# Expert loop of a Conformer and mixture-of-experts layer: where TensorE reads the expert classes, where the large experts stand in the sequence, and the order of TensorE's first turns

## The reference

```python
mod = silu(c) @ ada_w + ada_b                      # (1, 6*D): six vectors sh1, sc1, g1, sh2, sc2, g2
h = rmsnorm(x, mix_norm_g) * (1 + sc1) + sh1
u = h @ pw1_w + pw1_b; u = a * sigmoid(gt)         # a, gt: the halves of u
u = causal_depthwise_conv(u, dw_w, dw_b)           # 31 taps
y = silu(layernorm(u)) @ pw2_w + pw2_b;  x = x + g1 * y
h = rmsnorm(x, ffn_norm_g) * (1 + sc2) + sh2
top_val, top_idx = top_k(h @ router_w + router_b, 4)   # 4 of 32 experts for each token
for each expert e and its tokens xk:
    g, u = split(xk @ w1[e] + b1[e]);  act = (clip(u)+1) * (min(g,7) * sigmoid(1.702*g))
    y = act @ w2[e] + b2[e]                        # added to each token, weighted by its gate
x = x + g2 * moe;  out = rmsnorm(x, final_norm_g)
```

## Time and profile before

| what | value |
|---|---|
| device time, median of 3 runs | 1222.03 us (1221.42 to 1222.82) |
| device time of the profiled execution | 1223.35 us, of which 1221.5 us are the span from the first to the last instruction |
| TensorE matmuls busy | 1019.1 us, 83% of the span |
| DVE, ACT, POOL busy | 333.4, 165.4, 7.1 us |
| read from HBM | 455.9 MB, 374 GB/s over the span |
| chain of work that ended last | TensorE 64%, DMA 22%, issue 6%, DVE 5% |
| mean granted TensorE clock | 0.928 of full |

### The profile page before, as it was taken

The page is one execution under the profiler, slowest core; times in us unless marked ns, Lnnn a source line. Parts: engine busy times, 40 slices in busy tenths (PEclk is TensorE's granted clock), DMA queues, the critical chain, the costliest instruction groups (busy, mean ns, idle before and its releaser), DMA issues.

```text
span 1221.5 us, 20933 instructions
## 1 busy us (share of the span) xinstructions
PE 1019.1 (83%) x7648; PEld 476.7 (39%) x7649; DVE 333.4 (27%) x876; ACT 165.4 (14%) x364; POOL 7.1 (1%) x19
## 2 busy tenths in 40 slices
PE   3899994988899989998999799988787777877774
PEld 2577472333444334433443344333233323332321
DVE  3344457222113211231123112222121212121213
ACT  2233433010101010101010101010101010101001
POOL 1000000000000000000000000000000000000000
PEclk9999996899999988999999889989798989898988
DMA  9962990899999999999999998999999999999992
GB/s 353 280 276 102 334 389 19 335 421 421 421 395 386 421 422 382 374 422 422 414 382 421 422 409 339 422 423 423 421 422 421 423 421 422 422 422 422 422 421 110
DMA packets 84813, 457.39 MB, mean 374 GB/s; under 512 B 9497, under 2 KB 30097, under 8 KB 30993
## 3 DMA queue, kind: packets, MB, share of 16 engines
q1 hardware_dynamic: 83184, 456.29, 92.6%
q10 hardware_dynamic: 1600, 0.71, 0.2%
HBM read 455.93 MB, written 1.05 MB: 374 GB/s over the span
## 4 chain that ended last, share of the span: by engine, by line
PE 64%; DMA 22%; issue 6%; DVE 5%; ACT 1%; ACTq 1%; SPq 0%; DVEq 0%
PE bank L1226 29%; DMA ring<-in_exp_w 21%; PE bank L1249 15%; PE bank L1098 5%; PE bank L1205 3%; PE bank L1080 2%; PE bank L1119 2%; PE bank L1046 2%; PE bank L1217 2%; DMA xg<-in_conf_dw_w 1%; PE bank L1236 1%; DVE scratch L877 1%; PE bank L1203 1%; PE bank L1193 1%; DVE act L887 1%
## 5 line engine op out<-in xcount | busy, mean ns | idle before, releaser
L1226 PE MATMUL bank<-ring,xg 128*32 128x256 f32 (+2 forms) x3136 | 452.4, 484 | 42.9 <-DMA ring<-in_exp_w 42.6
L1226 PEld LDWEIGHTS bank<-ring,xg 128*32 128x32 f32 (+2 forms) x3136 | 175.2, 130 | 309.7 <-issue 206.0
L1249 PE MATMUL bank<-ring,actT 128*32 128x512 f32 (+2 forms) x1056 | 224.0, 622 | 24.2 <-DMA ring<-in_exp_w 16.1
L525 ACT ACTIVATE act<-scratch 128x128 f32<-128x128 f32 (+2 forms) x66 | 25.8, 391 | 810.2 <-DVE scratch L877 808.8
L1249 PEld LDWEIGHTS bank<-ring,actT 128*32 128x32 f32 (+2 forms) x1056 | 77.3, 135 | 147.6 <-issue 114.5
L866 DVE SCALAR_TENSOR_TENSOR acc<-bank,gate,acc 128x512 f32<-128x512 f32 x136 | 93.0, 744 | 81.0 <-PE bank L1205 71.8
L877 DVE TENSOR_SCALAR scratch<-bank 128x128 f32<-128x128 f32 (+2 forms) x66 | 25.6, 388 | 306.0 <-PE bank L1226 306.0
L896 DVE TENSOR_TENSOR ysb<-bank,g2half 128x512 f32<-128x512 f32 x29 | 20.1, 692 | 226.2 <-PE bank L1249 226.2
L1193 PEld LDWEIGHTS bank<-onehot_bf,arena 128*128 128x128 bf16 x1584 | 54.4, 100 | 22.0 <-issue 22.0
L1217 PE MATMUL bank<-b1s,bias_of 96*32 96x256 bf16 (+2 forms) x196 | 25.5, 375 | 43.6 <-issue 43.6
L1098 PE MATMUL bank<-hT,ring 128*128 128x256 f32 x256 | 58.6, 389 | 3.7 <-DVE wcol L645 3.7
(11 more groups left out here) (214 smaller groups left out, 513.1 us busy)
## 6 DMA issues: line engine op xcount, KB each, us to landing
ring<-in_exp_w SPq DMA_DIRECT2D x396, 1024.0 KB, 22.3
ring<-in_ada_w SPq DMA_DIRECT2D x24, 1024.0 KB, 9.9
ring<-in_conf_pw_w SPq DMA_DIRECT2D x12, 1024.0 KB, 11.4
acc<-in_x SPq DMA_DIRECT2D x1, 1024.0 KB, 5.0
out<-acc SPq DMA_DIRECT2D x2, 512.0 KB, 2.6
g2full<-in_ada_b SPq DMA_DIRECT2D x1, 512.0 KB, 4.6
xT<-in_final_norm_g ACTq DMA_DIRECT2D x1, 512.0 KB, 3.9
b1f<-in_exp_b SPq DMA_DIRECT2D x1, 256.0 KB, 4.2
```

The costliest lines, as they stand in the source:

```text
L525: a.activation(act[:, h * c:(h + 1) * c], g_lim[h][:, 0:c], ACT.Sigmoid, scale=ALPHA).then_inc(sig_ready, 1)
L1226: ins = mm(up_to(m, n, r), xg[:, b, k, 0:m], wk[:, at:at + span(m)], start=False, stop=(k == KT - 1))
L1249: ins = mm(dst, actT[:, f % (2 * q), at:at + m], wk[:, f % 2 * D + r * H:f % 2 * D + (r + 1) * H], start=(f < sides), stop=(f >= KT - sides))
```

## The change

- The first turns of TensorE are reordered: x is transposed ahead of the small vectors; the taps are transposed behind `turn_row(0)`, into bank 5 instead of bank 1; the first `pw1` matmul no longer waits for `v_dw`.
- TensorE enters the expert loop without `s_seq`. It reads two flags at the top of an iteration and one in each of its two items, behind the first two w1 chunks and behind a wait for `s_seq` at 1. The wait for 4 stands behind the loop.
- VectorE's `take_b2` moves from behind `eidx` to behind `extras`, ahead of the two last steps of `s_seq`.
- In the sequence the 5 largest experts go to positions 5, 11, 17, 23, 29, the next 5 to 3, 9, 15, 21, 27, and 5 more to 7, 13, 19, 25, 31. Before, the 7 largest stood at every second odd position from 5 on.

```diff
-        LATE = TOPS // 2
+        THIRD = TOPS // 3
...
             v.wait_ge(p_dw, 1)
-            v.tensor_copy(wcol[:, :, :, :], bank[1][:, 0:2 * P].rearrange(...)
+            v.tensor_copy(wcol[:, :, :, :], bank[5][:, 0:2 * P].rearrange(...)
...
-            late, early, rest_e = slice(0, LATE), slice(LATE, TOPS), slice(TOPS, E - 1)
-            for where, ranks, most_rows in ((slice(3, E + 1, 4), early, MIDDLE), (slice(5, E + 1, 4), late, MIDDLE),
-                                            (slice(2, E + 1, 2), rest_e, SMALL)):
+            for where, ranks, most_rows in ((slice(3, E + 1, 6), slice(THIRD, 2 * THIRD), MIDDLE),
+                                            (slice(5, E + 1, 6), slice(0, THIRD), MIDDLE),
+                                            (slice(7, E + 1, 6), slice(2 * THIRD, TOPS), MIDDLE),
+                                            (slice(2, E + 1, 2), slice(TOPS, E - 1), SMALL)):
...
             v.tensor_copy(extras[:, :], extra_n[:, :]).then_inc(s_seq, 1)
+            take_b2()
             link(v.tensor_scalar(first[:, :], iota_e[:, :], -1.0, float(E), ALU.mult, ALU.add))
...
             v.wait_ge(s_xcol, 1)
-            take_b2()
             v.wait_ge(dve, n[0])
...
             pe.wait_ge(s_const, 8)
-            pe.wait_ge(s_vec, 16 * 9)
-            tr(bank[0][:, 0:120], vrow[0:120, :], ident[0:120, 0:120]).then_inc(p_vec, 1)
             pe.wait_ge(s_x, 16)
             for k in range(KT):
...
                     ins.then_inc(p_x, 1)
+            pe.wait_ge(s_vec, 16 * 9)
+            tr(bank[0][:, 0:120], vrow[0:120, :], ident[0:120, 0:120]).then_inc(p_vec, 1)
...
-            pe.wait_ge(s_dw, 16 * 2 * STEPS)
-            for h in range(2):
-                ins = tr(bank[1][:, h * P:(h + 1) * P], dwrow[:, h, :, :].rearrange("p j c -> p (j c)"), ident[:, :])
-            ins.then_inc(p_dw, 1)
             pe.wait_ge(s_cwide, 1)
             pe.wait_ge(v_vec, 1)
             for k in range(KT):
                 ada(k)
             turn_row(0)
+            pe.wait_ge(s_dw, 16 * 2 * STEPS)
+            for h in range(2):
+                ins = tr(bank[5][:, h * P:(h + 1) * P], dwrow[:, h, :, :].rearrange("p j c -> p (j c)"), ident[:, :])
+            ins.then_inc(p_dw, 1)
...
-                if t == 0:
-                    pe.wait_ge(v_dw, 1)
...
-            def item(it, j, ws):
+            def class_at(at):
+                return pe.value_load(wide[0:1, bass.ds(at, 1)], min_val=0, max_val=1)
+
+            def item(it, j, prev, cur):
...
-                either(pe, ws[j + 1], SIZES[j], first)
+                either(pe, cur, SIZES[j], first)
+                pe.wait_ge(s_seq, 1)
+                after = class_at(it * UNROLL + (j + 2))
                 pe.wait_ge(y_ready, i + 1)
                 pe.wait_ge(acc_done, i2 + 1)
-                either(pe, ws[j], SIZES[1 - j], lambda m: scatter(1 - b, m))
+                either(pe, prev, SIZES[1 - j], lambda m: scatter(1 - b, m))
...
-                either(pe, ws[j + 2], SIZES[1 - j], lambda m: gather(1 - b, m))
+                either(pe, after, SIZES[1 - j], lambda m: gather(1 - b, m))
...
+                return after
...
             ins.then_inc(p_b2, 1)
+            with pe.Fori(0, E // UNROLL) as it:
+                prev, cur = class_at(it * UNROLL), class_at(it * UNROLL + 1)
+                for j in range(UNROLL):
+                    prev, cur = cur, item(it, j, prev, cur)
             pe.wait_ge(s_seq, 4)
-            with pe.Fori(0, E // UNROLL) as it:
-                ws = widths(pe, it)
-                for j in range(UNROLL):
-                    item(it, j, ws)
```

More of the change, by code:

```diff
@@ L644, in _ @@
             v.wait_ge(p_dw, 1)
-            v.tensor_copy(wcol[:, :, :, :], bank[1][:, 0:2 * P].rearrange("p (h q g) -> p h q g", h=2, q=STEPS)
+            v.tensor_copy(wcol[:, :, :, :], bank[5][:, 0:2 * P].rearrange("p (h q g) -> p h q g", h=2, q=STEPS)
                           ).then_inc(v_dw, 1)
@@ L1266, in first @@
                     up(i, b, m, range(2))
-                either(pe, ws[j + 1], SIZES[j], first)
+                either(pe, cur, SIZES[j], first)
+                pe.wait_ge(s_seq, 1)
+                after = class_at(it * UNROLL + (j + 2))
                 pe.wait_ge(y_ready, i + 1)
                 pe.wait_ge(acc_done, i2 + 1)
-                either(pe, ws[j], SIZES[1 - j], lambda m: scatter(1 - b, m))
-                either(pe, ws[j + 1], SIZES[j], lambda m: up(i, b, m, range(2, KT)))
+                either(pe, prev, SIZES[1 - j], lambda m: scatter(1 - b, m))
+                either(pe, cur, SIZES[j], lambda m: up(i, b, m, range(2, KT)))
                 pe.wait_ge(sel_ready, i * 5 + 10)
                 pe.wait_ge(acc_done, i2 + 3)
-                either(pe, ws[j + 2], SIZES[1 - j], lambda m: gather(1 - b, m))
+                either(pe, after, SIZES[1 - j], lambda m: gather(1 - b, m))
                 turn_onehot(1 - b)
                 pe.wait_ge(xg_ready, i + 2)
-                either(pe, ws[j + 1], SIZES[j], lambda m: down(i, i2, m))
+                either(pe, cur, SIZES[j], lambda m: down(i, i2, m))
+                return after
             pe.wait_ge(s_tab, 1)
```

## The result

The changed kernel takes 1195.54 us (median of 4 runs, 1193.06 to 1195.65) where the kernel before takes 1222.17 (4 runs beside it): ratio 0.9777, 95% interval 0.9764 to 0.9790. The profiled executions have spans of 1221.5 and 1193.8 us, so 27.7 us are to be found. The forecast had 21.8.

What follows compares the result with a forecast made beforehand. A serial front, then the experts' weight stream, slowed by TensorE at WIDE items, then a short tail bound the kernel. 10.1 + 6.5 + 5.2 = 21.8 us off 1223.35 gave 1201.5, median 1200; range 1193 to 1210.

Steps and rivals of the forecast that it cites:

- First turns: Ahead of the loop: ada follows the sums of squares directly, so pw1 starts at 32.8 instead of 42.86, 10.1 us.
- the stated risks: In the front: longer idle time ahead of the sums could slow them; low bound 7.2 us for the first turns.
- the bound of 6.9: In the front: the sums of squares could take anything from 3.5 to 6.9 us, against 5.38 before.
- Loop entry: At the start of the expert loop: TensorE and SP enter sooner, 6.5 us, between 4.8 (SP) and 7.0 (TensorE).
- the upper bound of 7.0: At the loop entry: TensorE's first matmul at 203.6, a gain of 7.0 us.
- Reads inside the items: Two reads less at an iteration's top: 1.3 us for each of four WIDE items, 5.2 us; bounds zero to 11.2.
- the drained ring: At WIDE items: the first matmuls run slow behind a ring of weight chunks that has emptied, then full.
- The high bound of 11.2: At WIDE items: 2.8 us each if shorter idle time also spares half of the slower first matmuls, taken as 1.5.
- Spacing: In the loop: WIDE items at positions 5, 11, 17, 23 instead of 5, 9, 13, 17; costed at nothing.
- The front's gain: Rival, stage loading expert 0: bound by bytes, so an earlier pw1 only makes TensorE wait; 1210 us, chance 0.12.
- The reads were not exposed: Rival, inside the items: reads not hidden, TensorE's sequencer empties the array at each; 1205 us, chance 0.13.
- The slower rival: At WIDE items: a read's pause keeps the clock low for the remaining 48 matmuls, 20.8 us each; 1283 us, chance 0.04.

Runs made afterwards that it cites:

- the two experiments: Kernel before with only TensorE's first turns reordered: 1209.26 us; changed kernel with the old order of first turns: 1205.22 us.
- the reads alone: Kernel before with only TensorE's reads moved, two flags at the top and one in each item; old wait, spacing and first turns: 1205.37 us.
- the reads at the top again: Changed kernel with TensorE reading all four flags at the top of each iteration and waiting for the sequence's first step ahead of the loop: 1206.4 us.
- The kernel with the filled pause: Changed kernel with all four reads at the top, plus 12 unused matmuls ending each TensorE iteration, run during the reads: 1199.82 us.
- the last two kernels: Changed kernel with old sequence and SP waiting only for the sequence's first step: 1189.72 us; same plus 24 unused matmuls ahead of the extra expert: 1191.78 us.
- one read more: Changed kernel with a third, unused read at the top of TensorE's iteration: 1196.9 us.
- the kernel with the filled tail: Changed kernel with old sequence and SP waiting only for the first step, plus 24 unused matmuls ahead of the extra expert: 1191.78 us.

## Why the prediction was right, and which of its terms were off

**First turns, 10.1 forecast.** Right: the order of events is as forecast, and pw1 moved by 9.3, with its first two tiles 1.5 quicker and the router's matmuls 1.7 slower; 9.1 were left at the loop, and 9.7 to 12.4 us by the two experiments' medians and ratios. The stretch ahead of the loop differs by some us between profiled runs with the same code there: with the old order in the changed kernel the last matmuls ahead of the loop start at 203.73, in the kernel before at 201.36. Of the stated risks one came true in part: the sums took 6.26 instead of 5.38, inside the bound of 6.9. Turning x first hardly moved the sums (17.82 against 18.01), as forecast. One step of the working is off by a chunk: TensorE reaches the last ada chunk seven chunks in and not six. The time given for it, 29.4, is that of seven, so nothing hangs on it.

**Loop entry, 6.5 forecast.** TensorE started 7.1 us sooner relative to its last matmuls (forecast 7.0), SP 4.5 (forecast 4.8). The fuller start of the stream gave 3.0 more, where 1.7 had been set down for it. So 7.5 in the profiled pair, a little above the upper bound of 7.0, which had counted only TensorE's own start. Two pairs of runs differ by the early entry and the spacing alone: the reads alone and the changed kernel with the old first turns (0.9879 and 0.9858), and the first turns alone and the reads at the top again (0.9905 and 0.9862). They give 2.6 and 5.3 us, each within about 4. On top of it come the reads that fall away at the entry itself; in the kernel with the reads alone SP started 1.7 sooner relative to the last matmuls. So the runs have 4 to 7 us for this term, in which the forecast lies, but they don't fix it.

**Reads inside the items, 5.2 forecast.** The mechanism was right, the size was not: 14.6 us in the profiled pair, 15.3 in the kernel with the reads alone. This is the term that was mis-sized. The late start was as reckoned, 1.6 us for each WIDE item against 1.5, 6.5 in all. But the lower clock behind the pause had been taken as a property of the drained ring, and its loss only into the upper bound, at 1.5 each. The kernel with the filled pause shows that it belongs to the pause: up to 2.6 us for each item (1.88 + 8.62 against 1.03 + 6.87). In the profiled pair the first 20 matmuls of the four items lost 9.2 us to it before and 1.7 after, so it makes 7.5 of the 14.6. The high bound of 11.2 for this term was too low, too. Its 1.5 was called half of what the slower matmuls lose, and is about all that the 16 lose (0.7 and 2.1); it left out the bias ahead of them, 1.88 against 1.03. The hidden reads inside the items were hidden, as forecast: no idle time stands ahead of a WIDE item's scatter.

**Spacing, nothing forecast.** Right: 1.0001 alone.

**What was missing.** The tail. It was not in the sum, and gave back 3.8 us in the profiled pair, nearly all of it at matmuls that ran at the lower clock. Its length from the last w2 chunk of position 32 was 53.4 us before, 52.8 to 53.9 in seven of the experiments, 54.8 and 55.8 in the last two kernels, and 56.7 to 57.4 in the changed kernel and three others. It followed no part of the change: one read more, or the first turns undone, made it short again. What sets it stays open.

**Luck.** That the time came out inside the range owes something to it. The reads gave 9.4 us more than forecast and the entry 1.0, the first turns 1.0 less, and the tail took back 3.8. Without the tail's loss the profiled execution would have taken 1191.8 us, below the range; the kernel with the old sequence, whose tail was short, took 1192.26.

**The rivals.** The front's gain was not given back. The reads were not exposed inside the items: the WIDE items got shorter by more than the top alone saves in reads. The slower rival, a clock that stays down inside an item, did not happen: the 48 matmuls behind the scatter took 20.81 in every WIDE item, and the changed kernel has a mean clock of 0.943 against 0.928. The Trainium skill's passage on small pauses between groups (TensorE: Matmul & The Clock Gate, A second HAM failure mode) would have had it go up and down; inside the WIDE items nothing of the kind was seen. It was the longer pause at the top that counted: behind a pause of 2.2 to 2.6 us the first matmuls were slow in 13 of 15 WIDE items (the kernel before, the first turns alone, the spacing alone, the reads at the top), behind one of 0.8 to 1.6 us in 5 of 37 (all other kernels without filler in the loop, and one item with the spacing alone). The Trainium skill (DMA: Bandwidth & Descriptors, Latency and other measured facts) gives a tensor_load a floor of about 600 ns. The trace does not agree, its loads take 0.30; and a floor says how little a read can cost, so it was no reason to put the term lower. The 0.77 from read to read was the better guide.

## What to carry to other kernels

Register reads at the top of a loop cost most where TensorE has just drained its queue: the array stands still while the sequencer reads, and then, in 13 items of 15 here, starts slowly. Move them behind matmuls that are already queued; where they can't be moved, something for the array to do during them gets back the clock, if not the start. When a pause ahead of work that sets the pace is shortened, price both, the start and the slow matmuls behind it, from the rows: compare the first matmuls behind the pause with the same ones later.

## What the runs showed of the hardware that I had not expected

The pause ahead of the extra expert is one branch. TensorE's sequencer in the kernel before, 1166 to 1180 us (ns min/median/max, first to last start):

```profile
L230 PEldq COMPARE_BRANCH  x2: 208/2856/5504, 1170.0 to 1172.6; - x2
```

The branch that starts at 1172.6 takes 5.5 us; the first matmul comes at 1178.12. In the kernel with the filled tail it takes 5.4 us and begins 1.8 us before the filler ends, so only 1.8 us of it are covered. Inside the loop no branch is like that from the second iteration on; one in the first iteration, at 253.8 us, took 3.45 (2.70 in the changed kernel). The same line of the kernel before, from 263 to 1168 us:

```profile
L230 PEldq COMPARE_BRANCH  x170: 70/202/215, 263.4 to 1163.2; - x170
```

The Trainium skill (Runtime: NRT & Kernel Launch, Instruction fetch mechanics) says that a taken branch whose target is not in the instruction window has to wait for a fetch. The trace agrees. From 263 to 1172.6 us the DMA queues moved no instruction packet at all; from 1172.6 to 1178.1, while the branch lasts, they moved one (packets, MB, share of the 16 DMA engines):

```profile
q8 instruction: 1, 0.02, 1.2%
```

So do they during the branch at 253.8 and during the long one in the changed kernel's tail. The packet itself was moved within 1 us (1175 to 1176); what the rest of the 5.5 us is, no row here shows. Nor is every first visit that dear: the other branches of the first iteration took 0.36 us or less.

The second is how little it takes to change the clock: the last 32 matmuls of the tail took 9.68 us in one kernel and 7.11 in another that differs from it in nothing but the order of experts.
